# Gathering experts beside a second token mixer taken in halves, with slots in all of its stages but the projections

## The reference

```python
mix = token_mixer(h, ...)                 # block 1: latent attention + a recurrence, gated, @ w_out
x = x + gt1 * mix
x = x + gt2 * peer_ffn(modulate(rms_norm(x)), ...)
...
proj = h @ w_in_2                         # block 2: fox (causal, forget gate), window and memory attention
x = x + (g0 * fox @ w_fox_o + g1 * swa @ w_swa_o + g2 * mem @ w_mem_o) @ w_out_2
x = x + peer_ffn_2(rms_norm(x), ...)
```

```python
u = take(expert_down, idx);  act = gelu(h . u)
v = take(expert_up, idx);    out += gate * act * v
```

## Time and profile before

| | |
|---|---|
| time, median of 3 runs | 5064.99 us (5050.13 to 5074.23) |
| the profiled execution | 5070.55 us, span 5068.7 us |
| mean granted TensorE clock | 0.843 |
| PE / DVE / ACT / Pool busy | 75 / 54 / 16 / 23% of the span |
| packets on Pool's queue | 1073.81 MB, 53.3% of 16 DMA engines |
| all other traffic | some 120 MB |

### The profile page before, as it was taken

One profiled execution on the slowest core, in us unless ns is written; L12 is line 12 of the kernel. 1 busy time (PEld: TensorE's weight loads), 2 busy tenths in 40 slices (PEclk: granted clock), 3 DMA queues, 4 the chain that ended last, 5 costly groups with the idle time before them and its releaser, 6 DMA issues. The chain is left out here.

```text
span 5068.7 us, 35703 instructions
## 1 busy us (share of the span) xinstructions
PE 3812.7 (75%) x11658; PEld 2123.6 (42%) x11658; DVE 2712.9 (54%) x5846; ACT 813.6 (16%) x2074; POOL 1174.9 (23%) x1028
## 2 busy tenths in 40 slices
PE   5945897775677777677779979788477777777777
PEld 4823796462233233233338734546223332322333
DVE  5558555346655656644443334533665565565454
ACT  1113001111111111111121212322111111111111
POOL 0000000002443444344410000000144334434443
PEclk9978787887888998888889955699788888988898
DMA  4500000127999999999952200122399999999998
GB/s 173 181 16 3 4 1 21 56 64 282 366 376 368 369 393 368 360 387 395 394 212 95 73 1 9 42 75 75 147 365 363 387 352 373 383 357 381 400 414 344
DMA packets 198993, 1194.16 MB, mean 236 GB/s; under 512 B 21642, under 2 KB 44426, under 8 KB 64914
## 3 DMA queue, kind: packets, MB, share of 16 engines
q0 software_dynamic: 147456, 1073.81, 53.3%
q1 hardware_dynamic: 51124, 118.42, 7.1%
q10 hardware_dynamic: 256, 0.02, 0.0%
HBM read 1190.04 MB, written 2.10 MB: 235 GB/s over the span
## 5 line engine op out<-in xcount | busy, mean ns | idle before, releaser
L1064 POOL DMA_INDIRECT e1g_pair<-in_experts,e1g_expert x512 | 585.7, 1144 | 1997.7 <-DVE e1g_expert L1196 1169.8
L1064 POOL DMA_INDIRECT e2g_pair<-in_experts,e2g_expert x512 | 589.0, 1150 | 1865.9 <-DVE e2g_expert L1196 1043.4
L1219 DVE CUSTOM_DVE_ANT_0 e2g_pair<-e2g_pair,e2g_hrow 128x1024 f32<-128x1024 f32 x512 | 626.4, 1225 | 601.6 <-DMA e2g_pair<-in_experts,e2g_expert 601.2
L1219 DVE CUSTOM_DVE_ANT_0 e1g_pair<-e1g_pair,e1g_hrow 128x1024 f32<-128x1024 f32 x512 | 626.8, 1225 | 598.8 <-DMA e1g_pair<-in_experts,e1g_expert 598.1
L1101 PE MATMUL e1g_acc<-e1g_pair,e1g_diag 128*128 128x512 f32 x1024 | 616.7, 688 | 425.2 <-ACT e1g_diag L1131 425.0
L1101 PE MATMUL e2g_acc<-e2g_pair,e2g_diag 128*128 128x512 f32 x1024 | 618.5, 689 | 422.7 <-ACT e2g_diag L1131 422.4
L1102 PE MATMUL e1g_acc<-e1g_pair,e1g_diag 128*128 128x512 f32 x1024 | 579.9, 651 | 0.0
L1102 PE MATMUL e2g_acc<-e2g_pair,e2g_diag 128*128 128x512 f32 x1024 | 579.0, 650 | 0.0
L1101 PEld LDWEIGHTS e1g_acc<-e1g_pair,e1g_diag 128*128 128x128 f32 x1024 | 210.1, 217 | 743.5 <-ACT e1g_diag L1131 460.1
L1101 PEld LDWEIGHTS e2g_acc<-e2g_pair,e2g_diag 128*128 128x128 f32 x1024 | 210.1, 217 | 739.6 <-ACT e2g_diag L1131 456.6
L1102 PEld LDWEIGHTS e2g_acc<-e2g_pair,e2g_diag 128*128 128x128 f32 x1024 | 219.2, 214 | 294.5 <-issue 294.5
(11 more groups left out here) (515 smaller groups left out, 4704.5 us busy)
## 6 DMA issues: line engine op xcount, KB each, us to landing
p_raw<-in_w_in SPq DMA_DIRECT2D x81, 512.0 KB, 3.5
p_w_ada<-in_w_ada SPq DMA_DIRECT2D x16, 1024.0 KB, 6.1
ada_w<-in_w_ada SPq DMA_DIRECT2D x4, 2048.0 KB, 10.6
po_raw<-in_w_out SPq DMA_DIRECT2D x16, 512.0 KB, 3.6
e1q_raw<-in_w_query SPq DMA_DIRECT2D x16, 512.0 KB, 3.5
e1g_pair<-in_experts,e1g_expert POOLq DMA_INDIRECT x512, 9.0
e2q_raw<-in_w_peer_q SPq DMA_DIRECT2D x16, 512.0 KB, 3.5
e2g_pair<-in_experts,e2g_expert POOLq DMA_INDIRECT x512, 8.9
```

What stands on the lines that cost most here:

```text
L1064: pool.indirect_dma_start(pair[n % BUFS][:], None, table, bass.IndirectOffsetOnAxis(ap=expert[:, t % 2, s:s + 1], axis=0)).then_inc(landed ...
L1219: ins = dve.tensor_tensor_reduce(pair[n % BUFS][:, 0:D], pair[n % BUFS][:, 0:D], hrow[:, t, :], 1.0, 0.0, ALU.mult, ALU.add, dot[:, t % 2, ...
```

## The change

The expert tables are split in two, `down` and `up` with rows of 4 KB. A slot now has two indirect DMAs, each 512 KB, into 6 down and 6 up buffers. The gather is an object, `Gather`, whose state outlives the stages, with one method for each engine that does beat n: Pool starts the down gather of slot n + 6 and the up gather of slot n - 15; DVE does the product of slot n; ACT gelu (in groups of 16) and the diagonal of slot n - 20; PE the two matmuls of slot n - 21. There are 1051 beats for the 1024 slots of both layers, in one row. Stages take a share of them (`Beats`) and lay them between their own instructions at so many points: an attention stage at its number of items plus 4, head norm at two for each chunk, the merge at its 24 units, a choice at its 21 pieces. `shared_out` divides a run of beats by the lengths given.

The order becomes: e1q, the first tile's choice c0 without slots; c1, the memory's stages, c23 with beats 0 to 283; then twice, for 256 tokens each, n3, p2, hn, vt, forget, foxa, swaa, mema, pg, mg, po, n4, q and a first choice, and a second one (c5, c7). p2, pg, po and q have length 0, so no slots stand in them; p2 is cut into 23 chunks and the gates' 24 (pg). The second half's queries see the first half's keys and values, kept in `Past`; the first half runs while the other tokens' part of layer 1 is gathered, the second half while the first half's part of layer 2 is. In hosting attentions the PSUM banks for scores go from 3 to 2 and those for outputs from 2 to 1. The memory's keys and values are stored to DRAM and loaded in each half, the alibi table and the second layer's keys are loaded inside the stages, once for each. The merge's weights come in rows of 2 KB. The rest of the beats, 810 to 1051, runs in `drain_stage`.

```diff
+GROUP, UBUFS, VBUFS, DIAGS = 16, 6, 6, 8
+TILES, SLOTS = 2 * TT, 2 * TT * NJ
+BENT_AT = GROUP + 1
+WEIGH_AT = BENT_AT + 1
+DIAG_AT = WEIGH_AT + 2
+UP_AT = DIAG_AT + 1
+BEATS = SLOTS + UP_AT + 6
...
+class Gather:
...
+    def pool(self, pool, n):
+        for m in range(0 if n == 0 else n + UBUFS, n + UBUFS + 1):
+            if m < SLOTS:
+                t, s = divmod(m, NJ)
+                if s == 0:
+                    pool.wait_ge(self.chosen, t + 1)
+                if m >= UBUFS:
+                    pool.wait_ge(self.dotted, m - UBUFS + 1)
+                pool.indirect_dma_start(self.down[m % UBUFS][:], None, self.layers[t // TT][0],
+                                        bass.IndirectOffsetOnAxis(ap=self.expert[:, t % TT, s:s + 1], axis=0)).then_inc(self.down_in[m % UBUFS], 16)
+        m = n - UP_AT + VBUFS
+        if 0 <= m < SLOTS:
+            t, s = divmod(m, NJ)
+            if m >= VBUFS:
+                pool.wait_ge(self.added, m - VBUFS + 1)
+            pool.indirect_dma_start(self.up[m % VBUFS][:], None, self.layers[t // TT][1],
+                                    bass.IndirectOffsetOnAxis(ap=self.expert[:, t % TT, s:s + 1], axis=0)).then_inc(self.up_in[m % VBUFS], 16)
...
+    def pe(self, pe, n):
+        m = n - UP_AT
+        if 0 <= m < SLOTS:
+            t, s = divmod(m, NJ)
+            pe.wait_ge(self.up_in[m % VBUFS], 16 * (m // VBUFS) + 16)
+            pe.wait_ge(self.diag_made, m + 1)
+            if s == 0 and t:
+                pe.wait_ge(self.kept, 2 * t)
+            up, diag = self.up[m % VBUFS], self.diag[m % DIAGS]
+            pe.matmul(self.acc[0][:], diag[:], up[:, 0:512], start=s == 0, stop=s == NJ - 1)
+            pe.matmul(self.acc[1][:], diag[:], up[:, 512:D], start=s == 0, stop=s == NJ - 1).then_inc(self.added, 1)
...
+    def act(self, act, n):
+        g, s = divmod(n - BENT_AT, GROUP)
+        if s == 0 and 0 <= g < SLOTS // GROUP:
+            t, q = divmod(g, NJ // GROUP)
+            at = slice(q * GROUP, (q + 1) * GROUP)
+            act.wait_ge(self.dotted, (g + 1) * GROUP)
+            act.activation(self.bent[:, t % 2, at], self.dot[:, t % 2, at], self.layers[t // TT][2]).then_inc(self.bent_made, 1)
+        m = n - DIAG_AT
+        if 0 <= m < SLOTS:
+            t, s = divmod(m, NJ)
+            act.wait_ge(self.weighed, m // GROUP + 1)
+            if m >= DIAGS:
+                act.wait_ge(self.added, m - DIAGS + 1)
+            act.activation(self.diag[m % DIAGS][:], self.k.ident[:], ACT.Copy, scale=self.weight[:, t % 2, s:s + 1]).then_inc(self.diag_made, 1)
...
+    def dve(self, dve, n):
+        g, s = divmod(n - WEIGH_AT, GROUP)
+        if s == 0 and 0 <= g < SLOTS // GROUP:
+            t, q = divmod(g, NJ // GROUP)
+            at = slice(q * GROUP, (q + 1) * GROUP)
+            dve.wait_ge(self.bent_made, g + 1)
+            dve.tensor_tensor(self.weight[:, t % 2, at], self.bent[:, t % 2, at], self.gate[:, t % TT, at], ALU.mult).then_inc(self.weighed, 1)
+        if n < SLOTS:
+            t, s = divmod(n, NJ)
+            down = self.down[n % UBUFS]
+            dve.wait_ge(self.down_in[n % UBUFS], 16 * (n // UBUFS) + 16)
+            dve.tensor_tensor_reduce(down[:], down[:], self.hrow[:, t % TT, :], 1.0, 0.0, ALU.mult, ALU.add,
+                                     self.dot[:, t % 2, s:s + 1]).then_inc(self.dotted, 1)
...
+class Beats:
...
+    def at(self, i):
+        return range(self.first + i * self.count // self.points, self.first + (i + 1) * self.count // self.points)
...
+def shared_out(gather, first, last, lengths):
+    whole, run, got = sum(lengths.values()), 0, {}
+    for name, length in lengths.items():
+        a, run = run, run + length
+        got[name] = Beats(gather, first + (last - first) * a // whole, first + (last - first) * run // whole)
+    return got
...
+    SC, PO = (2, 1) if hosting else (3, 2)
+    apart = PO == 2 or all(items[n][4] % per != items[n + 1][4] % per for n in range(N - 1))
+    beats = (beats or Beats()).over(N + 4)
...
+def second_mixer(nc, k, ins, cols, past, xT, hT, memory, half, beats):
+    own = lambda stage: f"{stage}h{half}"
+    now = slice(half * HALF, (half + 1) * HALF)
+    other = slice((1 - half) * HALF, (2 - half) * HALF)
+    first = half * HTILES
+    here = lambda t: slice((t - first) * P, (t - first + 1) * P)
+    x, h = xT[:, :, now], hT[:, :, now]
+    norm_stage(nc, own("n3"), k, x, DC, D, cols("norm1_g_2"), h, tokens=HALF, beats=beats["n3"])
...
+            project_stage(nc, own("p2"), k, ins["w_in_2"], h, DC, Y_GATE, z, tokens=HALF, beats=beats["p2"])
...
+        project_stage(nc, own("pg"), k, ins["w_in_2"][Y_GATE:Y_N], h, DC, 3 * DC, z, tokens=HALF, beats=beats["pg"])
+        merge_stage(nc, own("mg2"), z, 0, [(ins["w_fox_o"], foxT), (ins["w_swa_o"], swaT), (ins["w_mem_o"], memT)], h,
+                    bias=cols("b_gate_2"), tokens=HALF, beats=beats["mg"])
+    project_stage(nc, own("po2"), k, ins["w_out_2"], h, DC, DC, x, tokens=HALF, add=(k.ones, x), beats=beats["po"])
+    norm_stage(nc, own("n4"), k, x, DC, D, cols("norm2_g_2"), h, tokens=HALF, beats=beats["n4"])
...
+MIXER_LENGTHS = {"n3": 15, "p2": 0, "hn": 40, "vt": 8, "forget": 15, "foxa": 130, "swaa": 90, "mema": 40, "pg": 0, "mg": 70, "po": 0,
+                 "n4": 15, "q": 0, "choose": 90}
+def experts_and_second_mixer(nc, r, k, ins, cols, xT, hT, mod):
+    layers = [(ins["down1"], ins["up1"], ACT.Gelu_apprx_tanh, mod[:, 5 * DC:6 * DC]), (ins["down2"], ins["up2"], ACT.Gelu, None)]
+    gather = Gather(r, k, xT, layers)
+    memory = nc.dram_tensor("memory_scratch", [P, 8, NMEM], F32, kind="Internal").ap()
+    half_done = HTILES * NJ + UP_AT + 6
+    first_layer_done = TT * NJ + UP_AT + 6
+    keys_of_first = lambda c: c % 2
+    keys_of_second = lambda c: c
+    at = lambda t: (t, t % TT * P)
+    with ExitStack() as stack:
+        qT = Room(nc, stack, "e1").sb("qT", [P, 2 * PH, S])
+        project_stage(nc, "e1q", k, ins["w_query"], hT, DC, 2 * PH, qT)
+        choose_stage(nc, "c0", k, ins, gather, hT, qT, ins["keys1"], keys_of_first, [at(0)], [at(t) for t in range(TT)])
+        beats = shared_out(gather, 0, half_done, {"choose1": 62, "mn": 8, "mp": 50, "mh": 12, "mt": 4, "choose": 144})
+        choose_stage(nc, "c1", k, ins, gather, hT, qT, ins["keys1"], keys_of_first, [at(1)], [], beats=beats["choose1"])
+        memory_stages(nc, k, ins, cols, hT, memory, beats)
+        choose_stage(nc, "c23", k, ins, gather, hT, qT, ins["keys1"], keys_of_first, [at(2), at(3)], [], beats=beats["choose"])
+    past = Past(r)
+    starts = [half_done, first_layer_done]
+    ends = [TT * NJ - UBUFS, (TT + HTILES) * NJ - UBUFS]
+    for half in range(2):
+        t = TT + HTILES * half
+        beats = shared_out(gather, starts[half], ends[half], MIXER_LENGTHS)
+        second_mixer(nc, k, ins, cols, past, xT, hT, memory, half, beats)
+        h = hT[:, :, half * HALF:(half + 1) * HALF]
+        with ExitStack() as stack:
+            qT = Room(nc, stack, f"e2h{half}").sb("qT", [P, 2 * PH, HALF])
+            project_stage(nc, f"e2qh{half}", k, ins["w_peer_q"], h, DC, 2 * PH, qT, tokens=HALF, beats=beats["q"])
+            choose_stage(nc, f"c{t}", k, ins, gather, h, qT, ins["keys2"], keys_of_second, [(t, 0)], [(t, 0), (t + 1, P)], beats=beats["choose"])
+            choose_stage(nc, f"c{t + 1}", k, ins, gather, h, qT, ins["keys2"], keys_of_second, [(t + 1, P)], [],
+                         beats=Beats(gather, ends[half], starts[1] if half == 0 else ends[1] + 48))
+    drain_stage(nc, gather, Beats(gather, ends[1] + 48, BEATS))
...
-        peer(nc, "e1", k, ins, xT, hT, ins["w_query"], ins["keys1"], lambda c: c % 2, ins["experts1"],
-             ACT.Gelu_apprx_tanh, gain=mod[:, 5 * DC:6 * DC])
-        norm_stage(nc, "n3", k, xT, DC, D, cols("norm1_g_2"), hT)
-        second_mixer(nc, k, ins, cols, xT, hT)
-        norm_stage(nc, "n4", k, xT, DC, D, cols("norm2_g_2"), hT)
-        peer(nc, "e2", k, ins, xT, hT, ins["w_peer_q"], ins["keys2"], lambda c: c, ins["experts2"], ACT.Gelu)
+        experts_and_second_mixer(nc, r, k, ins, cols, xT, hT, mod)
...
-    a["experts2"] = np.concatenate([first("peer_u_2"), first("peer_v_2")], axis=1)
+    a["down2"], a["up2"] = first("peer_u_2"), first("peer_v_2")
...
-    for n in ("w_in", "w_in_2", "w_out", "w_out_2", "w_query", "w_peer_q", "w_mem_kv"):
+    for n in ("w_in", "w_in_2", "w_out", "w_out_2", "w_query", "w_peer_q", "w_mem_kv", "w_o_mla", "w_o_rwkv", "w_fox_o", "w_swa_o", "w_mem_o"):
```

More of the change, by code:

```diff
@@ L221, in finish, with norm_stage @@
         dve.tensor_tensor(self.mod[:, at], self.ps[:, 0:4 * self.groups], self.bcol[:, at], ALU.add)
[L224 removed]
+def norm_stage(nc, name, k, src, chunks, width, gain, dst, shift=None, tokens=S, beats=None):
+    beats = (beats or Beats()).over(2)
     with ExitStack() as stack:
@@ L1013, in _, with choose_stage @@
                         link(dve.tensor_tensor(out[:, m, :] if last else part[:, 0, :], part[:, 0, :], part[:, i, :], ALU.add))
```

(35 more changed lines are left out.)

523 lines of the change are left out of this document (296 added, 227 removed).

## The result

The changed kernel takes 5196.4 us (median; 5194.5 to 5211.3) where the kernel before takes 5067.9 (5050.1 to 5074.2): a ratio of 1.0258, 95% interval 1.0224 to 1.0292. Taken again with other kernels it gave 5201.7, ratio 1.0257 [1.0225, 1.0289]. The profiled execution took 5211.3, its span 5209.4.

The account below looks back on a forecast made before the run. Transfers bound the gather, PE and chains of small stages the 1020 us between. Summed: 1173 start, 824 beats 0 to 283, halves 846 and 925, projections 500, drain 633, store 10: 4911, so 4906 us; range 4680 to 5190.

Parts of the forecast that it names:

- The step that failed: Stage boundaries: Pool stands 30 us at entries in beats 0 to 283; projections 492 us, with barriers 500.
- the 16 us of twelve buffers: At the bare projections, the twelve buffers in flight go on landing, up to 16 us a break, credited with nothing.
- the longer items of the second half: Second half's foxa: items of 3.5 tiles, 10.5 us a step, adding 44 us.
- The value of 2.85 us: Cost of a slot with two 4 KB row gathers, taken from a range of 2.6 to 2.97; 1.425 us an issue.
- (a): Gather-bound parts: Pool's issues fall in step behind DVE's operations and transfers set 2.6 us a slot; 4775 us; chance 0.12.
- (b): Gather: nearly each DVE operation holds a Pool issue, 2.97 us a slot; 4980 us; chance 0.17.
- (c): 104 attention steps: in-order engines lay the host's chain bare, 3 us a step instead of 1, adding 208; 5115 us; chance 0.14.
- (d): Hosting attention stages: PE's clock stays at its lower level, 3.43 us a slot; 5290 us; chance 0.08.
- (e): Hosting stages: Pool's queue waits for PE before up gathers, so stages run as host plus slots; 5140 us; chance 0.06.
- 1.3 us a step to break even: Attention steps: 1.3 us beyond the 1 us counted outweighs the gain (5045 us).

Follow-up runs that it names:

- the kernel without drains: Changed kernel, GpSimd not drained at the end of stages that hold slots: 4834.5 us at first, 4926.6 us (ratio 0.9700) when taken again beside the changed kernel.
- the third set: Third of four sets of four kernels, each beside its own runs of the kernel before (here 5073.0 us); changed kernel 5201.7 us, the same without drains 4926.6.
- the PSUM experiment: Changed kernel, but in its last block alone DVE's product reads the token's row from PSUM instead of SBUF: 5206.7 us, ratio 1.0270.
- the first set: First of the four sets, where 4 KB row gathers went faster; kernel before 5074.1 us, changed kernel without drains 4834.5 us.

## Why the prediction was wrong

Cut at the same beats, in us; the kernel without drains is that of the third set, and the spans are 5209.4 and 4932.4 against a forecast of 4909:

| part | forecast | changed kernel | without drains |
| --- | --- | --- | --- |
| until the first beat | 1173 | 1183 | 1184 |
| beats 0 to 283 | 824 | 916 | 862 |
| first half with its bare projections | 846 + 250 | 1207 | 1080 |
| second half with its bare projections | 925 + 250 | 1252 | 1147 |
| from beat 810 to the end | 641 | 652 | 659 |

**The step that failed** is the one that says "At stage entries Pool stands ... 30" and, for the halves, has only 8 us "with barriers" beside the projections. It put the ends of stages at nothing. They cost 275 us: some 155 for Pool's arrears, the rest for landings and what else the drain does behind them. The step looked at how a stage begins and never asked what ends one once Pool's queue holds gathers that outlive it. The kernel before gave no sign: its gather fills a single block and waits for its landings itself. The code gave one, since every stage became a block with a Pool part. In rows of before the term could have been bounded: a gather in flight at the end of each of 28 stages, at up to the 16 us of twelve buffers (5.4 to 9.8 in fact) that the forecast itself names ("the twelve buffers in flight go on landing, up to 16 us a break, for which I credit nothing"). It saw the landings as a gain not counted; they were a wait.

**The rest of the sum stood.** Without the drains the kernel takes 4927 us, 21 from the forecast, though some of that is errors that cancel. First beat to last, in the changed kernel, foxa took 162 and 166 us (forecast 166 and 210: the longer items of the second half cost 5 and not 44), swaa 106 (128), mema 42 (60), mg 93 (113), c4 112 (122), n3 and n4 15 and 12 (22). From PE's first matmul to its last the projections took 73, 75, 27 and 51 in the first half (78, 81, 32 and 56 with their start). Entries and ends took what these left over even without drains: beats 0 to 283 are 38 us above, some 20 of them at the two memory blocks whose drains were left in.

**The slot.** The value of 2.85 us was met, 2.81 over the whole last block and 2.85 in 500 us of it, for a reason that was wrong. That is luck. I took transfers at half of an 8 KB packet, 2.6, and Pool's held issues as what lies above them; the PSUM experiment shows the transfers at 2.86 with no issue held. The Trainium skill's page "GPSIMD Engine Reference", section "Key points", says that GpSimd shares its SBUF interfaces with VectorE and contends with VectorE's instructions that have two SBUF inputs. The trace agrees: 1140 and 1007 ns fall to 937 when one input leaves SBUF. No time hangs on it in the changed kernel. What the split costs was mis-sized too: 0.16 us a slot in a gather with nothing hosted, where the forecast had 2.85 against 2.80.

**The rivals.** (a) wanted 2.6 us a slot and (b) 2.97, by fewer or more holds; it was 2.81 to 2.86 in the last block, with holds and without, so both fell for the changed kernel. What (a) describes did occur in the last block of three kernels of the first set: 2.57 us a slot, one issue in two held; but there Pool set the pace and not the transfers. (c): foxa was 162 and 166, not 206 and 250; it fell. (Its 1.3 us a step to break even leaves out 22 us; by its own sum, 5065 - 4906 = 159 over 104 steps, it is 1.5.) (d): the halves ran at a granted 0.89 and 0.90; it fell. (e), host plus slots, fell: hosting in the mixer is worth 201 us with drains and 424 without. The slower side was right, by a mechanism that none of them named.

## What to carry to other kernels

Before gathers, or any transfers issued by Pool, are spread over many blocks, look at what closes a block: a drain there makes all engines wait for Pool's arrears and for its transfers in flight, here 10 us at each of 28 ends. With the drains the mixer's slots bring 201 us, without them 424. In a block whose other engines are busy for longer than Pool's landings it costs nothing, as under the bare projections. If the data outlives the block anyway, let the engines meet on semaphores and wait for the landing where it is used; if the drain must stay, start Pool later so that it is through with the others. And when a comparison hinges on a few per cent, take both kernels in one set: a difference of 87 us between sets first passed for part of the cause.

## What the runs showed of the hardware that was not expected

- Pool's DRAIN at a block's end does not end before its gathers have landed: at all 28 ends the last packet ended 4.0 to 5.7 us behind the last issue and the DRAIN 0.8 to 4.6 us behind the packet, 5.4 to 9.8 in all. Where more gathers were in flight (the kernel that leaves out 13 drains, at its next projection) the packet came up to 10.9 us behind the last issue and the DRAIN 1.0 us behind the packet.
- The same 4 KB row gather ran at 408 GB/s steadily, at Pool's own pace, in three kernels of one set and at 361 to 370 in the other sets, with 0.3% and 3.5% of the rows taking 400 to 520 ns on average instead of 159. The kernel with 8 KB rows (309 ns as a rule in its one profile) took the same time in all sets.
- An issue of Pool that is held by DVE cost nothing where transfers were the bound: 50 us less Pool time in 500 us changed no time at all. At 2.57 us a slot, where Pool waits for nothing, it is part of the pace.
